# Stick-breaking attention in pairs of heads, with its mask and its sums in fp32r, inside a two-block transformer kernel

## The reference, cut to what matters

```python
def stick_breaking_attention(q, k, v):
    ...
        z = jnp.einsum('bqhd,bkhd->bhqk', qb, k).astype(jnp.float32) * scale
        mask = k_pos[None, :] < q_pos[:, None]
        log_beta = jax.nn.log_sigmoid(z)
        log_keep = jnp.where(mask, jax.nn.log_sigmoid(-z), 0.0)
        suffix = lax.cumsum(log_keep, axis=3, reverse=True) - log_keep
        a = jnp.where(mask, jnp.exp(log_beta + suffix), 0.0)
        return jnp.einsum('bhqk,bkhd->bqhd', a.astype(v.dtype), v)

def odd_mixer(h, positions, w_in, q_norm, kv_norm, w_uq, w_ukv, w_out):
    qc, kc, vc, c_q, c_kv, k_r = _split(h @ w_in, SPLIT_CD)
    o_c = stick_breaking_attention(...)
    q_full = heads(rmsnorm(c_q, q_norm) @ w_uq, H_MLA, NOPE_DIM + ROPE_DIM)
    kv_full = heads(rmsnorm(c_kv, kv_norm) @ w_ukv, H_MLA, NOPE_DIM + V_DIM)
    ...
    return jnp.concatenate([o_c, o_d], axis=-1) @ w_out
```

## Time and profile before

| what | value |
| --- | --- |
| time, median of 3 | 1098.76 us |
| time of the profiled execution | 1099.27 us |
| its span, first to last instruction | 1097.5 us |
| TensorE busy | 1067.2 us, 97% |
| TensorE weight loads | 934.0 us, 85% |
| VectorE busy | 680.7 us, 62% |
| ScalarE busy | 567.3 us, 52% |
| mean granted TensorE clock | 0.997 |
| HBM | 183.55 MB read, 168 GB/s over the span |

### The profile page before, as it was taken

The page is one execution under the profiler, slowest core; times in us unless marked ns, Lnnn a source line. Parts: engine busy times, 40 slices in busy tenths (PEclk is TensorE's granted clock), DMA queues, the critical chain, the costliest instruction groups (busy, mean ns, idle before and its releaser), DMA issues.

```text
span 1097.5 us, 17869 instructions
## 1 busy us (share of the span) xinstructions
PE 1067.2 (97%) x6692; PEld 934.0 (85%) x6692; DVE 680.7 (62%) x1048; ACT 567.3 (52%) x802; POOL 10.3 (1%) x15
## 2 busy tenths in 40 slices
PE   6999999999999999999999999999999999999996
PEld 5998877887999899897868999898988779889995
DVE  5797796766655655577675645655744766555553
ACT  5644744755644444454555544444645755544441
POOL 0000010000000000000000000000000000000000
PEclk9999999999999999999999999999999999999999
DMA  7754433565464566464334564565432335566531
GB/s 280 261 175 150 135 120 130 173 196 188 153 218 166 177 216 230 161 207 158 117 112 146 204 198 165 181 213 179 156 133 96 115 116 179 167 220 207 187 132 39
DMA packets 53658, 185.43 MB, mean 169 GB/s; under 512 B 5840, under 2 KB 9184, under 8 KB 53600
## 3 DMA queue, kind: packets, MB, share of 16 engines
q1 hardware_dynamic: 52544, 183.58, 50.6%
q10 hardware_dynamic: 1056, 1.06, 0.3%
HBM read 183.55 MB, written 1.07 MB: 168 GB/s over the span
## 4 chain that ended last, share of the span: by engine, by line
PE 82%; DVE 10%; ACT 4%; issue 2%; DMA 0%; DVEq 0%; SPq 0%; ACTq 0%
PE ps L402 25%; PE ps L404 25%; PE ps L403 25%; DVE wlo L1356 3%; PE ps L471 2%; ACT whi L947 1%; ACT arena L1008 1%; PE ps L544 1%; PE ps L520 1%; DVE arena L1425 1%; PE ps L595 1%; DVE arena L1479 1%; DVE stat L1478 0%; PE ps L843 0%; ACT arena L1018 0%
## 5 line engine op out<-in xcount | busy, mean ns | idle before, releaser
L1356 DVE TENSOR_TENSOR wlo<-raw,whi 128x1024 fp32r<-128x1024 f32 x339 | 405.9, 1221 | 189.3 <-ACT whi L947 188.1
L947 ACT ACTIVATE whi<-raw 128x1024 fp32r<-128x1024 f32 x339 | 348.6, 1053 | 193.2 <-PE ps L404 128.7
L402 PE MATMUL ps<-hT_hi,whi 128*128 128x256 f32 x1152 | 329.6, 286 | 0.1
L403 PE MATMUL ps<-hT_lo,whi 128*128 128x256 f32 x1152 | 326.6, 284 | 0.0
L404 PE MATMUL ps<-hT_hi,wlo 128*128 128x256 f32 x1152 | 326.5, 283 | 0.0
L402 PEld LDWEIGHTS ps<-hT_hi,whi 128*128 128x128 f32 x1152 | 221.5, 192 | 2.9 <-DVE hT_lo L1376 1.1
L403 PEld LDWEIGHTS ps<-hT_lo,whi 128*128 128x128 f32 x1152 | 221.6, 192 | 0.7
L404 PEld LDWEIGHTS ps<-hT_hi,wlo 128*128 128x128 f32 x1152 | 221.6, 192 | 0.0
L402 PE MATMUL ps<-whi,y_hi 128*128 128x512 f32 (+1 forms) x540 | 214.0, 396 | 0.7 <-DVE y_lo L1515 0.5
L404 PE MATMUL ps<-whi,y_lo 128*128 128x512 f32 (+1 forms) x540 | 209.9, 389 | 0.0
L403 PE MATMUL ps<-wlo,y_hi 128*128 128x512 f32 (+1 forms) x540 | 209.9, 389 | 0.0
(11 more groups left out here) (211 smaller groups left out, 749.9 us busy)
## 6 DMA issues: line engine op xcount, KB each, us to landing
raw<-stream SPq DMA_DIRECT2D x339, 512.0 KB, 4.2
x<-x_in SPq DMA_DIRECT2D x2, 512.0 KB, 3.7
arena<-scratch ACTq DMA_DIRECT2D x1, 1024.0 KB, 10.6
arena<-rb SPq DMA_DIRECT2D x1, 1024.0 KB, 6.3
bm<-decay SPq DMA_DIRECT2D x1, 1024.0 KB, 6.2
out<-x SPq DMA_DIRECT2D x4, 256.0 KB, 2.1
cst<-const SPq DMA_DIRECT2D x1, 906.0 KB, 10.5
arena<-gfin SPq DMA_DIRECT2D x1, 512.0 KB, 6.6
```

Of the source, the lines that this page charges most:

```text
L402: pe.matmul(o, a[0], b[0], start=start, stop=False)
L403: pe.matmul(o, a[0], b[1], start=False, stop=False)
L947: act.activation(whi[:, u % RING, :], raw[:, u % RAW, :], ACT.Copy).then_inc(sem("hi_done"), 1)
L1356: dve.tensor_tensor(wlo[:, u % RING, :], raw[:, u % RAW, :], whi[:, u % RING, :].bitcast(F32), ALU.subtract).then_inc(sem("lo_done"), 1)
```

## The change

Heads are worked in pairs p = 0 to 3, the latents `cq` and `ckv` come ahead of `sv`, and two kinds of products leave f32:

- `SB_SCORES = {8: 0, 11: 1, 14: 2, 17: 3}`: TensorE runs the scores of pair p after that unit, and its sums two units later (after 10, 13, 16, 19).
- the mask of both key blocks is one fp32r matmul of 256 columns per head, ahead of the scores, which add to it; the scores of the two heads follow one another.
- the softplus is split: ScalarE copies it to fp32r (`sbn_hi`), VectorE writes the rest (`sbn_lo`). The triangle of -1 is multiplied with each over 384 columns in fp32r; the block of -1 stays f32, 128 columns per head.
- the weights for the values get a place of their own for each pair (`sba`, in `bm`), and all values are computed in one block after unit 20, two heads in turn, into two banks, split in two halves.
- ScalarE makes fp32r copies of the identity, the mask and the triangle once, at u = 2.
- VectorE's `lo` of that step is placed between the min and the max of a pair, ScalarE's `hi` between the Ln and the new copy. The latents' norms, turns and splits are placed earlier.

```diff
-    for name, kind, cols, nkt in (("sq", "F", 512, KT), ("sk", "F", 512, KT), ("sv", "T", 512, KT),
-                                  ("cq", "T", 384, KT), ("ckv", "T", 288, KT), ("uq0", "T", 512, 3),
+    for name, kind, cols, nkt in (("sq", "F", 512, KT), ("sk", "F", 512, KT), ("cq", "T", 384, KT),
+                                  ("ckv", "T", 288, KT), ("sv", "T", 512, KT), ("uq0", "T", 512, 3),
...
+        SB_SCORES = {8: 0, 11: 1, 14: 2, 17: 3}
+        SB_SUMS = {u + 2: p for u, p in SB_SCORES.items()}
...
-                for c in (0, S):
-                    m = pe.matmul(ps[:, b, c:c + P], cs(C_ID), cs(C_ST), start=False, stop=True, skip_group_check=True)
+                for j in range(2):
+                    pe.matmul(c3(ps[:, W0 + j, :], a=2)[:, :, 0:P], unit_r, mask_r.unsqueeze(1).to_broadcast([P, 2, P]),
+                              start=True, stop=True)
+                for keys, queries in ((slice(0, P), slice(0, S)), (slice(P, S), slice(P, S))):
+                    at = keys.start + queries.start
+                    for j in range(2):
+                        g = slice(64 * j, 64 * j + 64)
+                        m = pe.matmul(ps[:, W0 + j, at:at + queries.stop - queries.start], sk[g, p, keys],
+                                      sq[g, p, queries], start=False, stop=True, skip_group_check=True)
                 m.then_inc(sem("sb_z"), 1)
...
+            def sb_sums(p):
+                for j in range(2):
+                    pe.wait_ge(sem("sb_nl"), 2 * p + j + 1)
+                    for n in (sbn_hi, sbn_lo):
+                        pe.matmul(ps[:, W0 + j, 0:3 * P], nsuf_r, n[:, j, :], start=False, stop=True,
+                                  skip_group_check=True)
+                for j in range(2):
+                    m = pe.matmul(ps[:, W0 + j, P:S], cs(C_NONE), sbn[:, j, S:S + P], start=False, stop=True,
+                                  skip_group_check=True)
+                m.then_inc(sem("sb_r"), 1)
...
+            def sb_values():
+                pe.wait_ge(sem("sb_a"), 4)
+                pe.wait_ge(sem("la_lo"), 2)
+                pe.wait_ge(sem("evac"), evac_no["sv"] + 1)
+                for p in range(4):
+                    at = (p % 2) * S
+                    for t, queries in ((0, slice(0, S)), (1, slice(P, S))):
+                        a = t * P + queries.start
+                        for j in range(2):
+                            g = slice(64 * j, 64 * j + 64)
+                            m = pe.matmul(ps[g, W2 + p // 2, at + queries.start:at + S],
+                                          sv[:, t, 128 * p + 64 * j:128 * p + 64 * j + 64],
+                                          sba[p][:, j, a:a + queries.stop - queries.start],
+                                          start=t == 0, stop=True, skip_group_check=True)
+                    if p % 2:
+                        m.then_inc(sem("sb_v"), 1)
...
-                if 11 <= u < 19:
-                    h = u - 11
-                    sb_sums(h)
...
-                    if h >= 1:
-                        sb_values(h - 1)
-                    if h < 7:
-                        sb_scores(h + 1)
+                if u in SB_SCORES:
...
+                    sb_scores(SB_SCORES[u])
+                if u in SB_SUMS:
+                    sb_sums(SB_SUMS[u])
+                if u == 20:
+                    sb_values()
...
+            def sb_round(p):
+                for j in range(2):
+                    act.wait_ge(sem("sb_n"), 2 * p + j + 1)
+                    act.activation(sbn_hi[:, j, :], sbn[:, j, :], ACT.Copy).then_inc(sem("sb_nh"), 1)
+
+            def sb_second(p):
+                act.wait_ge(sem("sb_r"), p + 1)
+                act.activation(sba[p], ps[:, W0:W0 + 2, 0:3 * P], ACT.Exp).then_inc(sem("sb_a"), 1)
...
+                if u - 1 in SB_SUMS:
+                    sb_second(SB_SUMS[u - 1])
...
+                if u - 1 in SB_SCORES:
+                    sb_first(SB_SCORES[u - 1])
...
                 hi(base + u + LEAD)
+                if u - 1 in SB_SCORES:
+                    sb_round(SB_SCORES[u - 1])
...
-                if u in (15, 18):
-                    la_squares(0 if u == 15 else 1)
+                if u in (11, 14):
+                    la_squares(0 if u == 11 else 1)
...
+            def sb_rest(p):
+                for j in range(2):
+                    dve.wait_ge(sem("sb_nh"), 2 * p + j + 1)
+                    dve.tensor_tensor(sbn_lo[:, j, :], sbn[:, j, :], sbn_hi[:, j, :].bitcast(F32),
+                                      ALU.subtract).then_inc(sem("sb_nl"), 1)
...
+                if u - 1 in SB_SCORES:
+                    lo(base + u + LEAD - 1)
+                    sb_second(SB_SCORES[u - 1])
+                    sb_rest(SB_SCORES[u - 1])
```

More of the change, by code:

```diff
@@ L248, in model @@
         sbt = c3(area(768), a=2)
+        sba = [c3(bm[:].rearrange("p a b -> p (a b)")[:, 768 * p:768 * p + 768], a=2) for p in range(4)]
         sbn = c3(area(768), a=2)
@@ L251, in model @@
         qTm = c3(arena[:, 0:2048], a=8)
+        unit_r = Y[0][:, 1, 3, 0:P]
+        mask_r = Y[0][:, 1, 3, P:S]
+        nsuf_r = Y[1][:, 1, 3, 0:P]
+        sbn_hi, sbn_lo = [c3(y[:, 0, 0:3, :].rearrange("p a b -> p (a b)"), a=2) for y in Y]
         rsB = kTd
@@ L299, in model @@
             c += {"M": NG, "O": 2}.get(JOBS[n]["kind"], 1)
-        la_at = [[(2 * pair_of["cq"] + k // 2, (k % 2) * S) for k in range(3)], [(W2, k * S) for k in range(2)]]
+        la_at = [[(W2 + k // 2, (k % 2) * S) for k in range(3)], [(W2, k * S) for k in range(2)]]
         latent = [[y[:, 1, 0:3, :] for y in Y], [h[:, 0:2, :] for h in hT]]
@@ L831, in lat @@
                 return f
[L833 to L841, removed]
-                for c in (0, S):
-                    m = pe.matmul(ps[:, b, c:c + P], cs(C_ID), cs(C_ST), start=False, stop=True, skip_group_check=True)
-                m.then_inc(sem("sb_z"), 1)
@@ L846, in sb_sums @@
[L846 to L867, removed]
+            def sb_scores(p):
+                if p >= 1:
+                    pe.wait_ge(sem("sb_a"), p)
+                else:
+                    pe.wait_ge(sem("sb_c"), 1)
+                for j in range(2):
[7 more added lines that the diff above has]
+                                      sq[g, p, queries], start=False, stop=True, skip_group_check=True)
+                m.then_inc(sem("sb_z"), 1)
@@ L879, in mla_turn @@
                     m.then_inc(sem("ml_tr"), 1)
-            seq = [(n, k) for n in ("sq", "sk", "sv", "cq", "ckv", "uq0", "uq1", "kn", "vn")
+            seq = [(n, k) for n in ("sq", "sk", "cq", "ckv", "sv", "uq0", "uq1", "kn", "vn")
                    for k in range(JOBS[n]["n"])]
@@ L897, in _ @@
                     spread_rs(2)
[L898 to L913 removed]
+                if u in SB_SCORES:
+                    if u == 8:
+                        pe.wait_ge(sem("evac_v"), evac_v_no["sk"])
+                    sb_scores(SB_SCORES[u])
[3 more added lines that the diff above has]
+                    sb_values()
+                if u in (15, 18):
+                    c = 0 if u == 15 else 1
                     pe.wait_ge(sem("la_n"), c + 1)
                     if c:
[L917 removed]
+                        pe.wait_ge(sem("la_lo"), 1)
                     for kt, (b, col) in enumerate(la_at[c]):
@@ L1833, in _, with sb_first, sb_second, sb_split @@
             n3 = JOBS["wob"]["u0"] - base
[L1834 to L1849, removed]
+            def sb_first(p):
+                dve.wait_ge(sem("sb_z"), p + 1)
+                for j in range(2):
+                    dve.tensor_scalar(sbt[:, j, :], ps[:, W0 + j, 0:3 * P], 30.0, None, ALU.min).then_inc(sem("sb_m"), 1)
+            def sb_second(p):
+                for j in range(2):
+                    dve.wait_ge(sem("sb_l"), 2 * p + j + 1)
+                    dve.tensor_tensor(sbn[:, j, :], sbt[:, j, :], ps[:, W0 + j, 0:3 * P], ALU.max).then_inc(sem("sb_n"), 1)
+            def sb_rest(p):
+                for j in range(2):
+                    dve.wait_ge(sem("sb_nh"), 2 * p + j + 1)
+                    dve.tensor_tensor(sbn_lo[:, j, :], sbn[:, j, :], sbn_hi[:, j, :].bitcast(F32),
+                                      ALU.subtract).then_inc(sem("sb_nl"), 1)
+            def sb_split(c):
+                dve.wait_ge(sem("sb_hi"), c + 1)
+                dve.tensor_tensor(Y[1][:, 0, 2 * c:2 * c + 2, :], c3(ps[:, W2 + c, :], a=2),
+                                  Y[0][:, 0, 2 * c:2 * c + 2, :].bitcast(F32), ALU.subtract).then_inc(sem("sb_lo"), 1)
             r64 = rot.rearrange("p t n -> p (t n)")
@@ L1863, in _ @@
             for u in range(n3):
[L1864 to L1869, removed]
-                    lo(base + u + LEAD)
[L1871 to L1875, removed]
+                if u - 1 in SB_SCORES:
+                    sb_first(SB_SCORES[u - 1])
+                if u in (16, 19):
+                    la_lo(0 if u == 16 else 1)
```

(14 more changed lines are left out.)

42 lines of the change are left out of this document (21 added, 21 removed).

## The result

The changed kernel takes 1084.17 us, the median of four runs (1083.90 to 1084.23), against 1098.68 before: a ratio of 0.9869, 95% interval 0.9851 to 0.9886. That is 14.5 us less, as the sum of the prediction had it.

The account below looks back on a forecast made before the run. TensorE was taken to bound the kernel (busy 97% of the span); 13.8 us of its work plus 0.7 of waits saved gave 14.5 us, so 1084.3 us, range 1082 to 1089 (within 1.7 us: 0.6).

Parts of the forecast that it names:

- Scores and mask: TensorE, per pair: fp32r mask and two heads' overlapping scores take 1.09 us against 2.64, saving 6.2 us in all.
- Sums: TensorE, per pair: fp32r triangle products and f32 block products take 1.14 us against 2.16, saving 4.1 us in all.
- Values: TensorE, one block for all pairs: two heads overlap on column halves, 2.8 us against 6.3, saving 3.5 us.
- Work together: TensorE's saved work over scores and mask, sums and values: 6.2 + 4.1 + 3.5 = 13.8 us.
- Waits: TensorE's waits in the stick-breaking stretch: 0.9 us after against 1.6 before, so 0.7 us saved.
- an earlier rotation: Layer's end: queries rotate earlier, as `la_lo` is no longer ahead; part of the better-than-walk rival, 1082 to 1083, chance 0.09.
- The prediction's own signs of being wrong: Pairs 2 and 3 wait too, scores wait for ScalarE's Exp, or the layer's end waits for something that came earlier before.
- The walk of the chain: From a pair's scores through ScalarE and VectorE to its sums: head 0's sums can start 4.7 us after the scores end.
- Neither engine became the limit: Rival: ScalarE or VectorE, in strict queue order, come late to pairs and become the limit; 1087.5 to 1090 us, chance 0.2.
- No part of the pairs failed to overlap: Rival: a pair's heads don't overlap in scores and values, 6.0 us come back, 1090.3 us; chance 0.08, whole or part.
- The clock did not fall: Rival: waits at sums and scores drop TensorE to 1.2 GHz, 1.7 us lost per stretch; 1100 or more, chance 0.03 (slower or nothing).
- the lateness at the layer's end: Sign of being wrong: the layer's end waits for something that came earlier before; no size given.

## Why the prediction was right, step by step

**Scores and mask**, 1.09 per pair: 1.17 to 1.18, and 1.29 at pair 2 with its wait, 4.8 in all for 4.4. Overlap and the price of fp32r were right; what lacked is the way onto the half array, some 0.1 us: the two masks take 0.32 to the first score, not 0.24 (0.11 to the second mask and 0.21 to the score). I had given the masks their bare distance, and counted the way back only.

**Sums**, 1.14: 1.07 where TensorE does not wait, 1.28 at pairs 0 and 1, where the first product of each head takes 0.28 and not 0.175 after a wait. 4.7 in all for 4.6.

**Values**, 2.8: 2.75. Two heads side by side on 256 columns, which no row had shown, overlap in full; the values' two heads write one bank, and the rule on banks in the Trainium skill, TensorEngine Tiling (Array Packing), Gotcha 1, takes nothing off here, as the rows said.

**Work together**: 12.3 us for 11.7, from 25.6 before for 25.5; saved 13.4 for 13.8.

**Waits**, 0.7 saved: 1.2. This term was wrong in both its parts, and by more than its own size in each. Before, I took 1.6 us from the view of waits. The idle time there begins when the last matmul's record ends, and the record (0.33 for 384 columns) outlasts the 0.175 to the next start by 0.16. By starts the eight gaps ahead of the sums were 2.8 us over the usual distances. Another 0.45 us of before is missing from my 1.6, as it lies behind the stretch that I priced: the first unit of `kn` waited for VectorE's part of the second latent (`la_lo`, 0.33 by starts, 0.17 by the view), and its own first product was slow by 0.1.

```profile
860.12 0.28 PE L404 MATMUL ps<-whi,y_lo 128*128 128x256 f32 x1
860.57 0.50 PE L402 MATMUL ps<-whi,hT_hi 128*128 128x512 f32 x1 [0.17 <-DVE hT_lo L1858]
```

This wait is gone: that part now ends at 838.55, and the unit begins at 844.97. After, by the same measure, the waits are 0.7 at the sums (0.46 and 0.21, walked as 0.4 and 0.4), 0.8 at the scores of pair 2 (I allowed 0.1) and 0.7 at the turn of the queries (I had none, and expected an earlier rotation): 2.2 where I had 0.9. So 0.6 came from these, 0.45 from the second latent, and 0.2 in small parts from ways onto the half array and the starts of other products. The prediction's own signs of being wrong were waits at pairs 2 and 3, scores that wait for the Exp, and a wait at the layer's end; the last two came. They did not show in the time. Against my sum, 1.3 us of waits more after were met by 1.8 more of before, and the work was 0.4 less. That 13.4 and 1.2 give the predicted 14.5 is luck, of misses with opposite signs.

**The walk of the chain** held: 4.7 us at pair 0; at pair 1 ScalarE, emptying and squaring `cq`, delayed the Exp to 1.06 us after the scores' last record ended (809.87 to 810.93), where I had 1.05. What I had sized wrong is ScalarE's queue behind it: I saw the norm of `cq` and a split ahead of the Exp, and took them to end in time. They ended 0.7 late.

**The rivals.** Neither engine became the limit. In the 43.6 us from the first scores to the end of the values VectorE is busy for 32.2 and ScalarE for 34.7 (I had 37 of 44 for ScalarE). The stream of weights needed more than the fifth that I gave it, 0.45 of DMA busy and 149 GB/s for 0.26 and 86, and no wait came of it:

```profile
799.20:842.80 43.60, 42.59 (x267) 36.41 (x265) 32.19 (x56) 34.66 (x65) 0.00 (x0) 1.00 0.45 149
```

No part of the pairs failed to overlap. The clock did not fall, but one unit less of cover would have brought it down twice. On the lateness at the layer's end, the prediction named the wrong sign: the copies of the values now wait for a block of values that comes later than any head's before, and the split behind them waits with them.

## What to carry to other kernels

Where a product uses half of TensorE's rows or columns, put its counterpart on the other half with at most three matmul instructions that must be passed (an f32 product is two); the second is then free, and the order within that reach is no matter. The cases run here are halves of the rows into two banks and halves of the columns into one. When products move to fp32r by a hi and lo split, price the chain that the split adds: here it gave back 1.9 of 2.3 us, and the waits behind it went when the Exp of pair 1 and the rounding copies were put ahead of splits of weights in ScalarE's queue. And in a queue that works in order, keep what waits behind what is urgent: each of the waits left here, at the sums, at the scores and at the turn, went when a split of weights changed sides with one or two instructions. And price a wait by starts, not by the idle time of a view.

## What the runs showed of the hardware

- Matmuls on different halves of the array do not start in program order: the fifth started with the first, the seventeenth with the thirteenth (which record is which is inferred from counts and distances). The Trainium skill, TensorE: Matmul & The Clock Gate, What overlaps and what doesn't, says that matmuls are strictly first in, first out in start and end; for matmuls on different row or column halves these traces differ, and the measurement decides.
- After a wait, the first product takes 0.1 us more to the second (0.28 for 0.175 at the sums of pairs 0 and 1).
- A step onto a half array costs about 0.1 us ahead of it (0.21 from the second mask to the first score, 0.11 between the masks) and 0.1 behind it (0.32 for 0.21 between the two passes of the first score), and a step off it as much (0.20 for 0.11 behind the last score, then 0.33 for 0.23). On the full array a step from f32 to fp32r products costs nothing in sum (0.03 for 0.11, then 0.31 for 0.23). The Trainium skill, TensorEngine Tiling (Array Packing), Key Properties, says that a change of the tiling mode drains TensorE; the traces agree, at about 0.2 us for each step.
- The clock fell after stretches with TensorE busy for 1.27 of 3.70 us and 1.77 of 3.46, and not after 1.06 of 3.42. The stretches are cut by hand, and in them the less busy one kept the clock, so from their busy shares alone one can't tell when it falls.
- An idle time in a view of waits starts at the end of the last matmul's record, so it is 0.16 us short of what the wait costs behind matmuls of 384 columns. Where a wait was removed, the layer moved by the distance of starts (0.82 for 0.84, 0.71 for 0.70) and not by the idle time (0.67, 0.54).
